# Two-block forward kernel: forgetting heads end transposed, X of the inverse by transposes, gate quarters and output projection spread

## The reference, cut to what matters

```
proj = u @ w_in                     # u = rmsnorm(h)
gq, gk, gv, gz, gb, ga, fq, fk, fv, ff = split(proj)
o_gdn = gated_delta(conv_silu(gq, gk, gv), beta(gb), decay(ga))   # 4 heads of 128
o_gdn = rmsnorm(o_gdn) * norm_w * silu(gz)
o_fox = forgetting_attention(fq, fk, fv, ff)                      # 8 heads of 64
h = h + concat(o_gdn, o_fox) @ w_out
```

## Time and profile before

| | us |
|---|---|
| median of 3 runs | 1049.89 (1049.25 to 1051.16) |
| the profiled execution, its own time | 1048.97 |
| its span, first to last instruction | 1046.6 |
| PE busy | 1014.1 (97%) |
| DVE busy | 610.6 (58%) |
| ACT busy | 475.2 (45%) |
| POOL busy | 113.0 (11%) |
| mean granted TensorE clock | 0.979 |

### The profile page before, as it was taken

One profiled execution on the slowest core, in us unless ns is written; L12 is line 12 of the kernel. 1 busy time (PEld: TensorE's weight loads), 2 busy tenths in 40 slices (PEclk: granted clock), 3 DMA queues, 4 the chain that ended last, 5 costly groups with the idle time before them and its releaser, 6 DMA issues.

```text
span 1046.6 us, 15998 instructions
## 1 busy us (share of the span) xinstructions
PE 1014.1 (97%) x6484; PEld 885.1 (85%) x6484; DVE 610.6 (58%) x859; ACT 475.2 (45%) x830; POOL 113.0 (11%) x117
## 2 busy tenths in 40 slices
PE   8999999999999999999999998999999799999996
PEld 7988777879989999987787896978878689999885
DVE  4963566368856656666544779634323467576542
ACT  6334455356445434545444666332324254444332
POOL 1000120001300001013200042211200000110000
PEclk9999999999999999999999999899989899999999
DMA  8745434545556642420154442220002246555450
GB/s 301 266 135 188 161 130 177 181 174 183 177 187 245 240 159 96 147 82 1 41 189 173 161 161 92 100 92 1 1 1 81 80 166 213 170 197 189 174 201 40
DMA packets 23340, 150.54 MB, mean 144 GB/s; under 512 B 3532, under 2 KB 3800, under 8 KB 5864
## 3 DMA queue, kind: packets, MB, share of 16 engines
q1 hardware_dynamic: 22960, 149.39, 40.8%
q10 hardware_dynamic: 312, 0.18, 0.1%
HBM read 148.50 MB, written 1.05 MB: 143 GB/s over the span
## 4 chain that ended last, share of the span: by engine, by line
PE 91%; DVE 3%; ACT 2%; DMA 1%; issue 1%; SPq 1%; POOL 0%; ACTq 0%; POOLq 0%; DVEq 0%
PE psum L671 88%; DMA ring<-in_weights 1%; PE psum L750 1%; PE psum L1065 1%; DVE ring_parts L1855 1%; DVE R L2137 1%; ACT high_parts L1461 0%; ACT R L1468 0%; PE psum L1071 0%; PE psum L1232 0%; SPq L612 0%; DVE xT_parts L523 0%; ACT PTb L1704 0%; PE psum L1194 0%; PE psum L1236 0%
## 5 line engine op out<-in xcount | busy, mean ns | idle before, releaser
L1855 DVE TENSOR_TENSOR ring_parts<-ring,high_parts 128x1024 fp32r<-128x1024 f32 (+1 forms) x272 | 332.9, 1265 | 182.9 <-ACT high_parts L1461 182.1
L1461 ACT CAST high_parts<-ring 128x1024 fp32r<-128x1024 f32 x268 | 267.9, 1050 | 224.8 <-PE psum L671 186.8
L671 PE MATMUL psum<-xT_parts,high_parts 128*128 128x256 f32 (+1 forms) x960 | 218.0, 286 | 1.5 <-DVE ring_parts L1855 1.0
L671 PE MATMUL psum<-xT_parts,ring_parts 128*128 128x256 f32 (+1 forms) x672 | 193.0, 287 | 0.0
L671 PE MATMUL psum<-high_parts,xT_parts 128*128 128x512 f32 (+1 forms) x560 | 182.5, 403 | 6.6 <-DVE xT_parts L523 6.6
L671 PE MATMUL psum<-high_parts,R_parts 128*128 128x512 f32 (+1 forms) x560 | 167.5, 374 | 2.2 <-DVE R L2352 1.1
L671 PEld LDWEIGHTS psum<-xT_parts,high_parts 128*128 128x128 f32 x960 | 163.9, 190 | 2.6 <-DVE ring_parts L1855 1.2
L671 PE MATMUL psum<-R_parts,high_parts 128*128 128x256 f32 x832 | 160.6, 281 | 0.0
L671 PEld LDWEIGHTS psum<-high_parts,xT_parts 128*128 128x128 f32 (+1 forms) x560 | 104.3, 188 | 33.6 <-issue 8.9
L671 PEld LDWEIGHTS psum<-R_parts,high_parts 128*128 128x128 f32 x832 | 131.7, 188 | 0.1
L671 PEld LDWEIGHTS psum<-xT_parts,ring_parts 128*128 128x128 f32 x672 | 127.4, 190 | 0.1
(11 more groups left out here) (288 smaller groups left out, 1128.0 us busy)
## 6 DMA issues: line engine op xcount, KB each, us to landing
ring<-in_weights SPq DMA_DIRECT2D x136, 1024.0 KB, 4.9
h<-in_x SPq DMA_DIRECT2D x4, 256.0 KB, 4.8
ring<-in_weights SPq DMA_DIRECT2D x4, 256.0 KB, 6.7
G<-in_gains SPq DMA_DIRECT2D x2, 512.0 KB, 7.1
out<-xn SPq DMA_DIRECT2D x2, 512.0 KB, 3.1
R<-in_ret_tabs SPq DMA_DIRECT2D x1, 768.0 KB, 12.0
tab<-in_tabs SPq DMA_DIRECT2D x1, 663.5 KB, 6.1
G<-in_p_t SPq DMA_DIRECT2D x1, 512.0 KB, 7.0
```

The source lines that it names most:

```text
L671: return pe.matmul(out, lhsT, rhs, start=first, stop=last, skip_group_check=True)
L1461: act.copy(as_r(hi), value).then_inc(sem("units_high"), 1)
L1855: return dve.tensor_tensor(as_r(value), value, value_of(hi), ALU.subtract)
```

## The change

- `Q` loses the bank `be`. Its four spread matmuls open the group of bank `bq`; ACT takes the exponential of that bank, and only then does the new item `Qm` let PE add the mask (with a new wait on `query_exp`) and ACT take the second exponential.
- In the levels above 1, `Lz` also transposes Y into a bank `x`, and DVE copies it to X. The product and the subtraction for X go.
- c is split into three bf16 rows per head: DVE writes the first, and two more into a scratch that ACT moves to partitions 8 to 23 by two DMAs. A matrix `of_head_3` of 24 rows, formed once near the masks, selects and adds them in one bf16 matmul.
- A new item `Fn`: DVE scales Pf by the reciprocal sums before the transposes. `Fo` has the values of two heads as stationary operand and PfT as moving operand, so its output has channels on the partitions; ACT writes the high part of 64 rows and DVE the low part straight into the source of the output projection. `H` and `mT1` go.
- The order of the items is rewritten: two more `fin` ahead of `ss`, the `fv` blocks between `Q`, `Qm` and `kv`, three of the four `gz` blocks inside the levels, and the upper half of the output projection as two items `mo`, one ahead of the last chunk's output (`Vo`, 2) and one behind it.

```
 def mixer_order():
 
-    order = [("fin", 0), ("ss",), ("fin", 1), ("fin", 2), ("fin", 3), ("tok",), ("A", 1), ("A", 2), ("fin", 4), ("A", 0)]
-    order += [("Lz", 0, c) for c in level_chunks(0)] + [("fin", j) for j in (5, 6, 7)]
-    order += [("fv", half, c) for half in range(2) for c in range(3)]
-    beside = {1: ([("Q", 1), ("Fs", 0)], [("Q", 2), ("kv", 1)]), 2: ([("Fs", 1)], [("Ft", 0), ("Fs", 2)]),
-              3: ([("kv", 2), ("Ft", 1)], [("Fo", 0), ("Fs", 3)]), 4: ([("Ft", 2), ("Fo", 1)], [("Fs", 4), ("kv", 0)]),
-              5: ([("Ft", 3), ("Fo", 2)], [("Fs", 5), ("Ft", 4)]), 6: ([("Fo", 3), ("Fs", 6)], [("Ft", 5), ("Fo", 4), ("Fs", 7)])}
+    order = [("fin", 0), ("fin", 1), ("fin", 2), ("ss",), ("fin", 3), ("fin", 4), ("fin", 5), ("tok",), ("fin", 6), ("A", 1),
+             ("A", 2), ("fin", 7), ("A", 0)] + [("Lz", 0, c) for c in level_chunks(0)]
+    order += [("fv", 0, 0), ("Q", 1), ("fv", 0, 1), ("Qm", 1), ("Q", 2), ("fv", 0, 2), ("Qm", 2), ("kv", 1), ("fv", 1, 0),
+              ("kv", 2), ("fv", 1, 1), ("Fs", 0), ("fv", 1, 2), ("kv", 0)]
+    beside = {1: ([("Fn", 0), ("Fs", 1)], [("Ft", 0)]), 2: ([("Fn", 1), ("Fs", 2)], [("Fo", 0), ("Ft", 1)]),
+              3: ([("Fn", 2), ("gz", 0, 0)], [("Fs", 3), ("Fo", 1)]), 4: ([("Fn", 3), ("Ft", 2), ("Fs", 4)], [("gz", 0, 1)]),
+              5: ([("Fn", 4), ("Fo", 2), ("Ft", 3)], [("Fs", 5), ("Fo", 3)]),
+              6: ([("Fn", 5), ("Ft", 4), ("Fs", 6)], [("gz", 1, 0), ("Fn", 6), ("Fo", 4), ("Ft", 5)])}
     for n in range(1, len(LEVELS)):
         order += [("Lz", n, c) for c in level_chunks(n)] + beside[n][0]
         order += [("Lx", n, c) for c in level_chunks(n)] + beside[n][1]
-    order += [("W", 1), ("Ft", 6), ("W", 2), ("Fo", 5), ("gz", 0, 0), ("Vn", 0), ("Ft", 7), ("gz", 0, 1), ("Vo", 0),
-              ("Fo", 6), ("gz", 1, 0), ("Vn", 1), ("Fo", 7), ("gz", 1, 1), ("Vo", 1), ("Vn", 2), ("Vo", 2), ("H",)]
+    order += [("W", 1), ("Fs", 7), ("W", 2), ("Fo", 5), ("Vn", 0), ("Fn", 7), ("Ft", 6), ("Vo", 0), ("gz", 1, 1), ("Vn", 1),
+              ("Fo", 6), ("Ft", 7), ("Vo", 1), ("Fo", 7), ("Vn", 2), ("mo", 0), ("Vo", 2), ("mo", 1)]
     return order
...
         elif kind == "Lz":
-            u += [(("z", *at), "act" if n else "dve")]
+            u += [(("z", *at), "act" if n else "dve")] + [(("x", *at), "dve")] * (n > 1)
         elif kind == "Lx":
-            u += [(("y", *at), "dve")] + ([] if last_level(*at) else [(("x", *at), "dve")])
+            u += [(("y", *at), "dve")]
         elif kind == "Fs":
             u += [(("fs", n), "act")]
         elif kind == "Ft":
             u += [(("fT", n), "act"), (("fm", n), "dve")]
         elif kind == "Fo":
-            u += [(("fo", n), "act")]
+            u += [(("fo", n), "dve")]
         elif kind == "W":
             u += [(("gw", n), "act")]
         elif kind == "Vn":
             u += [(("vn", n), "act")]
         elif kind == "Vo":
             u += [(("go", n), "act")] * (n > 0) + [(("st", n), "dve")] * (n < 2)
-        elif kind == "H":
-            u += tr_uses("mT1", 2, 2)
     return u
...
+        negc = ctx.enter_context(nc.sbuf_tensor("negc", [3 * FH, TM], BF16))[:, :]
+        of_head_3 = ctx.enter_context(nc.sbuf_tensor("of_head_3", [3 * FH, FH], BF16))[:, :]
+        negc_parts = R[0:FH, R3 + 8 * TM + 1536:R3 + 9 * TM + 1536].bitcast(BF16)
+
+        def fox_out(k):
+
+            return R[:, R4 + 2048 + k * T:R4 + 2048 + (k + 1) * T], R[:, R2 + 8 * TM + k * T:R2 + 8 * TM + (k + 1) * T]
+
+        def fox_out_of(hd):
+            return tuple(part[hd % 2 * FD:hd % 2 * FD + FD, :] for part in fox_out(hd // 2))
+
         for n, (name, buf, c0) in enumerate([("W", Pf, 0), ("lnb", Pf, TM), ("UQ", Pf, 2 * TM), ("Lk", R, R2 + 12 * TM + 192),
                                              ("Lq", R, R2 + 13 * TM + 192)]):
...
-                bank = aux.open(pe, ("be", c))
+                bank = aux.open(pe, ("bq", c))
                 for hd in range(GH):
                     ins = mm(bank[:, hd * n:(hd + 1) * n], ident[0:4, hd:hd + 1].to_broadcast([4, P]),
-                             SM["UQ"][:, t0:t0 + n], True, True)
-                aux.full(ins, ("be", c))
-                bank = aux.open(pe, ("bq", c))
-                spread_rows(bank, n, "UQ", c)
-                aux.full(masked(bank, c, causal_b, ident_b), ("bq", c))
+                             SM["UQ"][:, t0:t0 + n], hd == 0, False)
+                ins.then_inc(sem("query_rows"), 1)
                 bank = aux.open(pe, ("qk", c))
                 for hd in range(GH):
                     ins = mm(bank[0:n, hd * n:(hd + 1) * n], ch(4 + hd, t0, n), ch(hd, t0, n), True, True)
                 aux.full(ins, ("qk", c))
+
+            def query_mask(c):
+                pe.wait_ge(sem("query_exp"), c)
+                aux.full(masked(aux.at(("bq", c)), c, causal_b, ident_b), ("bq", c))
 
             def fox_scores(hd):
...
+                    mm(o, of_head_3[:, hd:hd + 1].to_broadcast([3 * FH, P]), negc[:, 0:n], False, False)
                     ins = mm(bank[:, at_ + n - P:at_ + n], ident_b, causal_b, False, True)
                     at_ += n
...
                 p = Pf[:, hd % 2 * 416:hd % 2 * 416 + 416]
-                wait_read(pe, aux, ("fs", hd))
+                pe.wait_ge(sem("fox_scaled"), hd + 1)
                 bank = aux.open(pe, ("fT", hd))
                 for n, c0 in enumerate((M, P + 2 * M, 2 * P + 2 * M)):
...
-                    v0 = R3 + 8 * TM + c * 512 + hd * FD
-                    return R[0:m, v0:v0 + FD]
-
-                for b in range(TT):
-                    o = bank[:, b * FD:(b + 1) * FD]
-                    mm(o, PfT[0:M, slot + 384 + b * P:slot + 384 + (b + 1) * P], v(0, M), True, False)
-                    for k in range(b + 1):
-                        ins = mm(o, PfT[:, slot + (b + k) * P:slot + (b + k + 1) * P], v(1 + k, P), False, k == b)
+                    v0 = R3 + 8 * TM + c * 512 + hd // 2 * P
+                    return R[0:m, v0:v0 + P]
+
+                mm(bank[:, 0:T], v(0, M), PfT[0:M, slot + 384:slot + 384 + T], True, False)
+                mm(bank[:, 0:T], v(1, P), PfT[:, slot:slot + T], False, False)
+                ins = mm(bank[:, P:T], v(2, P), PfT[:, slot + T:slot + T + P], False, True)
                 aux.full(ins, ("fo", hd))
 
             state, v_new = R1 + 3072, R1 + 3584
 
-            def turn_mix(half):
-
-                for f in (2 * half, 2 * half + 1):
...
+                return tuple(part[:, c0 - M:c0 - M + m] for part in fox_out(k - 4))
+
+            def mix_output(half, c):
+
+                w, product = next_unit(4)
+                for t in range(TT):
+                    bank = main.open(pe, ("mo", c, t)) if half else main.at(("mo", c, t))
+                    if half and (c, t) == (0, 0):
+                        wait_read(pe, aux, ("fo", FH - 1))
+                    if half == 0 and (c, t) == (1, 1):
+                        turn_ffn(0)
+                    for k in range(4):
+                        ins = parts3(product, bank, mix_src(4 * half + k, *rows[t]), w(k, slice(0, 512)),
+                                     half == 1 and k == 0, half == 0 and k == 3)
+                    if half == 0:
+                        main.full(ins, ("mo", c, t))
 
             unit = {}
 
...
+                    if lv > 1:
+                        bank = aux.open(pe, ("x", lv, c))
+                        for hd in range(GH):
+                            ins = pe.transpose(bank[0:n, hd * n:(hd + 1) * n], mat(PTb, C_ALL, c, hd), ident[0:n, 0:n])
+                        aux.full(ins, ("x", lv, c))
                 elif kind == "Lx":
                     lv, c = key
                     wait_read(pe, aux, ("z", lv, c))
                     if lv > 1:
-                        wait_read(pe, aux, ("x", lv - 1, c))
+                        wait_read(pe, aux, ("x", lv, c))
                     n = CHUNKS[c][1]
                     z = z_rows(c)
                     bank = aux.open(pe, ("y", lv, c))
                     for hd in range(GH):
                         ins = mm(bank[0:n, hd * n:(hd + 1) * n], mat(PTb, 0, c, hd), of_head(z, c, hd), True, True)
                     aux.full(ins, ("y", lv, c))
-                    if not last_level(lv, c):
-                        bank = aux.open(pe, ("x", lv, c))
-                        for hd in range(GH):
-                            ins = mm(bank[0:n, hd * n:(hd + 1) * n], of_head(z, c, hd), mat(PTb, 0, c, hd), True, True)
-                        aux.full(ins, ("x", lv, c))
                 elif kind == "W":
                     c = key[0]
                     wait_read(pe, aux, ("y", len(LEVELS) - 1, c))
...
-                        if half == 0:
-                            main.full(ins, ("mo", c, t))
+            pe.wait_ge(sem("mix_ready"), 2)
+            turn_mix()
+            for c in range(2):
...
+                    act.wait_ge(sem("query_rows"), c)
```

(47 more changed lines are left out.)

62 lines of the change are left out of this document (22 added, 40 removed).

## The result

The changed kernel takes 1024.01 us in the median of four runs (1022.64 to 1025.62); the kernel before took 1049.57 beside it (1044.24 to 1051.16). The ratio is 0.9774, with a 95% interval of 0.9748 to 0.98: 2.3% faster. The forecast was 1018.5 us, 5.5 too low, and the range of 1006 to 1032 holds the result. The profiled execution took 1022.64 us, 26.3 less than the profiled one of before (1048.97).

The account below looks back on a forecast made before the run. TensorE (PE), busy for nearly the whole span, was taken as the bound. Savings of 14.1 us work, 7.4 waits and 9.6 clock sum to 31.1, taking 1048.97 to 1017.9, or 1018.5 on the median's scale; range 1006 to 1032.

Parts of the forecast that it names:

- case 1: The forecast itself: PE's stream shrinks and the clock half recovers; 1011 to 1025 us, chance 0.58.
- The X part: In the levels, transposes of Y replace the fp32 products for X on PE; 4.8 us saved.
- The query rows' 2.0: The second copy of the UQ rows goes, 16 passes in all on PE; 2.0 us saved.
- the turns' 0.9: The high half of the output no longer needs its eight turns on PE; 0.9 us saved.
- (a): First query bank, behind level 0's z for chunk 1, which DVE frees after the forgetting rows; a wait of 1.8 us.
- (b): Projection ahead of the last chunk, until DVE reads head 7 behind chunk 1's norm; a wait of 1.4 us.
- (c): Stage end: a weight unit's low part on DVE precedes the turned output's low parts; wait of 2.2 us, 1.6 before.
- the small ones: Five small PE waits in the mixer stage, 3.5 us together before the change; 1.6 us expected to remain.
- Rival 4: Slower: the clock sits at its lower level through the levels, where X passes become transposes; 1073 us, chance 0.05.
- Rival 3: Levels become round trips, the X copy between z and y on DVE: twelve waits of 0.8 us; 1028 us, chance 0.12.
- Rival 2: The clock gives nothing back: as many stretches at 1.2 GHz, at other places; 1028 us, chance 0.17.
- Rival 5: More than forecast: heads' values follow closely (4.6 us) and most of the clock returns (7 us); 1007 us, chance 0.08.

Follow-up runs that it names:

- e4: Changed kernel with the heads' work moved ahead of the level 6 gate block and the gates' rows made after DVE's level 0 z subtractions; 1014.1 us.
- b2: Changed kernel with gate blocks still in the levels but after the heads' work, the projection's halves together and the gates' rows later; 1010.7 us.
- u2: Changed kernel with the forgetting rows again as one fp32 matmul of eight rows, without the split into three and the DMAs; 1029.5 us.

## Why the prediction was right, and where it missed

The forecast's case 1 came out: PE's stream shrank and part of the clock came back. Of the 31.1 us, 26.3 arrived in the profiled execution (25.5 of them in the stage).

The errors partly cancel: work came out 1.9 us better, waits 3.1 and clock 4.4 worse. At 1024.0 the time is also just inside the 1025 of case 1.

**Work: 14.1 forecast, 16.0 measured.** The X part stands: four transposes take 0.44 us (the step from 734.48 to 734.92 below), as the earlier trace rows had it; undoing it costs 4.7 to 7.1 us. The query rows' 2.0 and the turns' 0.9 were not undone by themselves. Two terms were mis-sized, and the timeline of PE, as the earlier trace rows, shows both:

```profile
729.52 0.23 PE L677 MATMUL psum<-negc,of_head 24*128 24x144 bf16 x1
729.69 0.23 PE L677 MATMUL psum<-causal_b,ident_b 128*128 128x128 bf16 x1
...
730.50 0.28 PE L677 MATMUL psum<-negc,of_head 24*128 24x272 bf16 x1
730.72 0.23 PE L677 MATMUL psum<-causal_b,ident_b 128*128 128x128 bf16 x1
730.88 1.54 PE L677 MATMUL psum<-PfT,R 16*128 16x256 f32 x6
732.26 1.06 PE L677 MATMUL psum<-PTb,G 128*128 128x128 f32 x8
...
734.48 0.60 PE L1368 MATMUL psum<-tab,PTb 128*128 128x128 f32 x4
734.92 0.49 PE L1239 MATMUL psum<-tab,Pf 128*128 128x128 f32 x3
```

The bf16 rows take 0.17 + 0.22 = 0.39 us per head, not 0.3: eight heads save 5.7, not 6.4. The values of a head take 732.26 - 730.88 = 1.38 us. I took 1.7, nothing saved, with 1.1 as the other end; 0.3 per head is 2.4 us more. So the sum is 4.8 + 2.0 + 5.7 + 2.4 + 0.9 = 15.8, beside the 16.0 of the windows. "I take 0, since the scores' passes are nearest" was the wrong choice: the true price was about half way to the other end.

**Waits: 7.4 forecast, 4.3 measured.** The three places named are there. (a) The first query bank waits 2.0 us (1.8), behind the scan and the rows on DVE; moving these removed it. (b) The upper half of the projection waits 1.85 (1.4). (c) The last low parts wait 2.0 (2.2). For the small ones 1.6 was kept and 1.4 is there, but that is luck: none of the five is left, and the 1.4 ahead of `tok` is a new wait that the prediction doesn't have. The step that failed is **"In the levels I find no new wait"**. I had looked at z, X and y, whose engines were in time, and they are: no level product waits. But 2.9 us stand at their end, ahead of head 7's scores. I had counted the weight unit's 2.36 us on DVE only against the levels' own work. Its low part falls between a gate block and the read that frees a bank used four places before, and the bank is the head's, not the level's.

**Clock: 9.6 forecast, 5.2 measured.** The low clock after 820 is gone, as is the one at 701 and in the levels. Two falls took their place: 3.0 us behind wait (a), which I had foreseen as a wait but given no clock, and 7.7 behind the wait of head 7. The prediction listed the idle 5.0 us as a cause of low clock, and then priced its own new waits at their length alone. The filled waits show that the price is more: with PE kept busy, the same lateness loses 5.9 us less clock at head 7 and 3.2 less at the query bank.

**The rivals.** Rival 4 (the clock at its lower level in the levels, because of the transposes) is refuted: 1.00 with and without them. Rival 3 (round trips in the levels) has no row for it. Rival 2 (clock lost as before, elsewhere) came true in kind and by half in size: the falls from 640 to 670, at 701, in the levels and after 820 are gone, and about 11 us are lost at two other places. Rival 5 was half right: the values of the heads were cheaper, the clock was not.

**Parts that don't pay.** The forecast priced the moved gate blocks and the first projection at 0 and asked only what they would cover. In the levels they weren't needed as cover, and they set the order in which ACT and DVE reach the heads' banks. The moved projection brought a wait of 1.85 us and saved one of 0.7, and the wait at the end is 0.4 longer with it, not shorter. Together with the late query bank that is the difference between 1024.0 and 1008.2 us.

What stays open: why the clock falls in some stretches with waits of 0.4 us or none (765 to 775 in e4 and b2, 745 to 765 in u2), and why behind the waits ahead of `tok`, (b) and (c) it falls in one execution and not in another. No run here separates the passes' width from what came before them.

## What to carry to other kernels

With rotating banks, ask of each opened bank who reads its use four places earlier, and what is queued on that engine ahead of the read: an inserted block moves this for every user of the group, not only for its neighbours. Price a new wait of PE of two or three microseconds at its length plus what the clock may lose behind it, and test that by filling the wait with unread passes: this tells the clock's part from the lateness without moving anything. Don't read a fall of the clock in one profile as the effect of an edit before you have looked at what the same stretch does in other executions, best in kernels that are the same up to there. Work moved as cover into levels that had no long wait only cost here, so move first what the trace shows to be waiting.
